# A hybrid decoder block: weight splits three tiles ahead for longer, nine attention units turned a slot later, sums of squares two slots behind the output

## The reference, cut to what matters

```python
u = rms_norm(h, norm1_w)                       # h: 16 meta tokens + 256 tokens, width 1024
proj = einsum('bld,dn->bln', u, w_in)          # a_q a_k a_v d_q d_k d_v d_gate d_beta d_a gate_a gate_d
y_a = differential_attention(a_q, a_k, a_v, lambdas, subln_w, lambda_init)
y_d = gated_deltanet(d_q, d_k, d_v, d_gate, d_beta, d_a, conv_w, A_log, dt_bias, norm_w)
mixed = sigmoid(gate_a) * (y_a @ w_branch_attn) + sigmoid(gate_d) * (y_d @ w_branch_dn)
h = h + mixed @ w_out
h = h + hierarchical_moe(rms_norm(h, norm2_w))  # 32 experts, the weights of all of them are read
out = rms_norm(h, final_norm_w)[:, 16:]

# differential attention, 8 heads, value width 128, blocks of 128 queries:
p = softmax(s + bias)                          # two maps per head
w = p[:, :, 0] - lam * p[:, :, 1]
o = einsum('bhqk,bkhe->bqhe', w, v)
o = rms_norm(o, subln_w) * (1 - lambda_init)   # needs the sum of squares of o per head and query
# DeltaNet inputs: d_q, d_k, d_v pass a causal convolution of 4 taps and SiLU
```

## Time and profile before

| | |
|---|---|
| median of 3 runs | 667.23 us (667.16 to 667.66) |
| the profiled execution | 665.98 us |
| its span in the profile | 664.2 us |
| TensorE busy | 601.6 us, 91% |
| VectorE busy | 327.4 us, 49% |
| ScalarE busy | 268.4 us, 40% |
| read from HBM | 154.12 MB |
| mean granted clock of TensorE | 0.972 |

### The profile page before, as it was taken

The page is one execution under the profiler, slowest core; times in us unless marked ns, Lnnn a source line. Parts: engine busy times, 40 slices in busy tenths (PEclk is TensorE's granted clock), DMA queues, the critical chain, the costliest instruction groups (busy, mean ns, idle before and its releaser), DMA issues.

```text
span 664.2 us, 14323 instructions
## 1 busy us (share of the span) xinstructions
PE 601.6 (91%) x5931; PEld 507.3 (76%) x5931; DVE 327.4 (49%) x693; ACT 268.4 (40%) x598; POOL 55.6 (8%) x102
## 2 busy tenths in 40 slices
PE   8999999899998799999999999999999677785874
PEld 8999989798988788899899999997554433444451
DVE  5344476878877568564765388624112110110112
ACT  6245567667776745333533575423110010100003
POOL 8300011101000002100220040000000000000000
PEclk9799999899999899999999999999999988997999
DMA  9744543233335331121312159999989999999994
GB/s 289 238 160 160 175 141 106 88 127 128 128 127 191 127 127 65 66 66 64 126 53 80 64 189 341 421 419 418 421 354 420 421 421 423 421 423 420 421 409 158
DMA packets 68560, 156.04 MB, mean 235 GB/s; under 512 B 4818, under 2 KB 54116, under 8 KB 56596
## 3 DMA queue, kind: packets, MB, share of 16 engines
q1 hardware_dynamic: 67136, 154.89, 61.4%
q0 software_dynamic: 176, 0.17, 0.2%
q10 hardware_dynamic: 1188, 0.12, 0.2%
HBM read 154.12 MB, written 1.05 MB: 234 GB/s over the span
## 4 chain that ended last, share of the span: by engine, by line
PE 45%; DMA 10%; SPq 9%; DVE 6%; ACT 5%; issue 3%; DVEq 0%; ACTq 0%
PE bank L850 19%; DMA arena<-in_expert_w_gate_dram 8%; SPq L521 6%; PE bank L1261 6%; PE bank L1037 5%; PE bank L835 3%; SPq L616 2%; DMA arena<-in_expert_w_down_dram 2%; PE bank L1015 2%; PE bank L1242 2%; PE bank L1286 1%; PE bank L1297 1%; DVE ring_lo L338 1%; ACT w_hi L333 1%; DVE arena L1909 1%
## 5 line engine op out<-in xcount | busy, mean ns | idle before, releaser
L850 PE MATMUL bank<-uT_hi,w_hi 128*128 128x272 f32 (+1 forms) x568 | 170.1, 299 | 4.6 <-ACT arena L1430 3.3
L850 PE MATMUL bank<-uT_lo,w_hi 128*128 128x272 f32 (+1 forms) x568 | 163.9, 289 | 0.0
L850 PE MATMUL bank<-uT_hi,ring_lo 128*128 128x272 f32 (+1 forms) x568 | 163.7, 288 | 0.0
L338 DVE TENSOR_TENSOR ring_lo<-arena,w_hi 128x1024 fp32r<-128x1024 f32 x88 | 107.6, 1226 | 48.0 <-ACT w_hi L333 47.4
L850 PEld LDWEIGHTS bank<-uT_hi,w_hi 128*128 128x128 f32 x568 | 109.1, 192 | 8.1 <-ACT w_hi L333 3.5
L850 PEld LDWEIGHTS bank<-uT_lo,w_hi 128*128 128x128 f32 x568 | 109.2, 192 | 0.2 <-issue 0.2
L850 PEld LDWEIGHTS bank<-uT_hi,ring_lo 128*128 128x128 f32 x568 | 109.2, 192 | 0.0
L333 ACT ACTIVATE w_hi<-arena 128x1024 fp32r<-128x1024 f32 x88 | 92.0, 1051 | 0.8 <-DMA arena<-in_w_in_dram 0.7
L1261 PE MATMUL bank<-arena 128*32 128x256 f32 x1024 | 63.7, 405 | 20.9 <-DMA arena<-in_expert_w_gate_dram 20.9
L1261 PEld LDWEIGHTS bank<-arena 128*32 128x32 f32 x1024 | 35.2, 116 | 44.4 <-issue 22.3
L1909 DVE SCALAR_TENSOR_TENSOR arena<-arena 128x272 f32<-128x272 f32 x72 | 36.0, 500 | 18.0 <-ACT arena L1423 17.4
(11 more groups left out here) (368 smaller groups left out, 1033.6 us busy)
## 6 DMA issues: line engine op xcount, KB each, us to landing
arena<-in_w_in_dram SPq DMA_DIRECT2D x36, 1024.0 KB, 5.0
arena<-in_expert_w_gate_dram SPq DMA_DIRECT2D x32, 1024.0 KB, 25.9
arena<-in_expert_w_up_dram SPq DMA_DIRECT2D x32, 1024.0 KB, 22.7
arena<-in_expert_w_down_dram SPq DMA_DIRECT2D x29, 1024.0 KB, 21.9
arena<-in_w_branch_attn_dram SPq DMA_DIRECT2D x4, 1024.0 KB, 5.1
arena<-in_w_branch_dn_dram SPq DMA_DIRECT2D x4, 1024.0 KB, 5.1
arena<-in_w_out_dram SPq DMA_DIRECT2D x4, 1024.0 KB, 8.4
arena<-in_expert_w_down_dram SPq DMA_DIRECT2D x6, 512.0 KB, 18.6
```

Of the source, the lines that this page charges most:

```text
L338: nc.vector.tensor_tensor(low_of(SPLIT[q]), src, w_hi[HI_OF[q]].bitcast(F32), ALU.subtract).then_inc(w_lo_ready, 1)
L850: last = pe.matmul(ps[:, 0:b.shape[2]], a[:, c, :], b[:, c, :], start=(c == 0 and i == 0), stop=(c == NC - 1 and i == 2))
```

## The change

Splits run three tiles ahead for n from 16 to 53 instead of 16 to 42. The fifth home serves until tile 55 instead of 44, and a tile takes the home whose last use is longest ago. The first expert load into slot 9 moves from behind unit 28 to behind unit 34. `out_high` waits for the last yd tile that used the homes in its area: tiles 80, 80, 88 and 87 done instead of 80, 80, 86 and 88.

Units 7 to 15 are turned three slots behind their own instead of two, and multiplied by the values four slots behind instead of three; units 0 to 6 stay. Keep and square of a head go with its output. The sums of squares come two slots behind the output instead of one.

```diff
-LONG_LEAD = range(FIRST["aq"], FIRST["dv"] + 3)
+LONG_LEAD = range(FIRST["aq"], FIRST["gate"] + 6)
...
-HI_OF = [q % (NSPLIT + 1) if q < FIVE_UNTIL else q % NSPLIT for q in range(len(SPLIT))]
+HI_OF = []
+for q in range(len(SPLIT)):
+    homes = range(NSPLIT + 1 if q < FIVE_UNTIL else NSPLIT)
+    HI_OF.append(min(homes, key=lambda i: max([p for p in range(q) if HI_OF[p] == i], default=i - NSPLIT - 1)))
...
+        TURN_SLOT = [m + (2 if i < 7 else 3) for i, m in enumerate(UNIT_SLOT)]
+        OUT_SLOT = [m + 1 for m in TURN_SLOT]
...
         def head_at(m):
-            i = unit_at(m)
+            i = unit_at(m, OUT_SLOT)
...
-                if u == FIRST["gate"] // 2 + 4:
+                if u == FIVE_UNTIL // 2 + 6:
...
-                if unit_at(m - 2) is not None:
-                    att_turn(unit_at(m - 2))
+                if m in TURN_SLOT:
+                    att_turn(unit_at(m, TURN_SLOT))
...
-                if unit_at(m - 3) is not None:
-                    att_out(unit_at(m - 3))
-                if head_at(m - 4) in (3, 7):
-                    att_ss(head_at(m - 4) // 4)
+                if m in OUT_SLOT:
+                    att_out(unit_at(m, OUT_SLOT))
+                if head_at(m - 2) in (3, 7):
+                    att_ss(head_at(m - 2) // 4)
...
-                if unit_at(m - 2) is not None:
-                    tr_out(("w", unit_at(m - 2)))
+                if m in TURN_SLOT:
+                    tr_out(("w", unit_at(m, TURN_SLOT)))
...
-                if head_at(m - 3) is not None:
-                    att_sq(head_at(m - 3))
+                if head_at(m) is not None:
+                    att_sq(head_at(m))
...
-                act.wait_ge(tile_ready, FIRST["yd"] + (0, 0, 6, 8)[i])
+                users = [n for n in SPLIT if HI_OF[n] < NSPLIT and HI_OF[n] // 2 == OUT_HI[i] - TSLOTS]
+                act.wait_ge(tile_ready, users[-1] + 1 if users else FIRST["yd"])
...
-                if head_at(m - 3) is not None:
-                    att_keep(head_at(m - 3))
+                if head_at(m) is not None:
+                    att_keep(head_at(m))
```

More of the change, by code:

```diff
@@ L381, in hybrid_block, with unit_at @@
         FIRST_SLOT = UNIT_SLOT[0]
-        def unit_at(m):
-            return UNIT_SLOT.index(m) if m in UNIT_SLOT else None
+        TURN_SLOT = [m + (2 if i < 7 else 3) for i, m in enumerate(UNIT_SLOT)]
+        OUT_SLOT = [m + 1 for m in TURN_SLOT]
+        def unit_at(m, slots=UNIT_SLOT):
+            return slots.index(m) if m in slots else None
         def head_at(m):
-            i = unit_at(m)
+            i = unit_at(m, OUT_SLOT)
             return i // TT if i is not None and i % TT == TT - 1 else None
@@ L403, in hybrid_block @@
         for m in range(FIRST_SLOT, SLOTS_A):
-            if unit_at(m - 2) is not None:
-                TR.append(("w", unit_at(m - 2)))
+            if m in TURN_SLOT:
+                TR.append(("w", unit_at(m, TURN_SLOT)))
             if m >= 16 + 2 and m - 2 < 24:
@@ L950, in key_sums @@
                 if 11 <= m <= 11 + H:
-                    turned = [key for key in TR if key[0] == "v" or key[0] == "w" and UNIT_SLOT[key[1]] + 2 < m or key[0] == "dv" and key[1] + 18 < m]
+                    turned = [key for key in TR if key[0] == "v" or key[0] == "w" and TURN_SLOT[key[1]] < m or key[0] == "dv" and key[1] + 18 < m]
                     pe.wait_ge(tr_copied, len(turned))
```

## The result

The changed kernel takes 658.73 us (median of four runs, 657.65 to 661.15), the kernel before 667.19 us beside it (four runs, 665.83 to 667.66): 8.5 us less by the medians. The ratio formed over all runs is 0.9883, interval [0.9856, 0.9910], which is 7.8 us less. The profiled execution took 661.15 us with a span of 659.4 us, so it is the slowest of the four.

A forecast was written before the change was run, and what follows sets the result against it. TensorE was taken to bound the kernel up to about 450 us, expert weight loads after. 5.2 + 1.24 - 1.0 - 0.4 = 5.0 us off the median 667.23 gave 662.2 us, range 659.8 to 664.6.

The forecast's parts named there:

- The ring does not get shorter: Rival, ScalarE and VectorE in the slots: ring stays at 4.21 us a slot; gain 3.3 us, 663.9 us; chance 0.18.
- The expert stage swallows it: Rival, expert stage: first loads bound by bandwidth, not finished tiles, so nothing comes through; 667.2 us; chance 0.05.
- Two short waits make one long one: Rival, dv turns: two waits of about a microsecond in one slot bring half clock; 1.5 us less gain, 663.7; chance 0.12.
- Parts 1 and 2: Slots with turns and sums of squares: waits of 1.73 and 1.97 us and 1.5 us of half clock go, 5.2 us.
- Part 2: Sums of squares two slots behind the output: the 1.97 us wait and 1.5 us of half clock behind it go.
- Part 3: dv turns, slots 18 and 19: dv 1 waits as before, dv 0 may wait too; 1.0 us lost.
- a ring that lags: At the dv turns: ScalarE and VectorE lag TensorE more than before, so the high end, 1.0 us lost, was taken.
- Part 4: Splits three tiles ahead until the sixth gate tile: two waits for low parts in slots 22 to 25 go, 1.24 us.
- Part 1: Units 7 to 15 turned a slot later: three waits before turns go, 1.73 us; ring needs about 4.0 us a slot.
- Part 5: Output tiles: third w_out copy waits for all eight yd tiles and delays the last mix copy; 0.4 us lost.
- its own low end: Whole kernel: nothing lost at the dv turns and the old 1.0 us there gone too; 7.4 us less, 659.8 us.

The follow-up runs named there:

- late_keep: Changed kernel with keep and square of a head a slot later, in slots without scores, and sums a slot later too; 664.42 us, ratio 0.9967.
- turn_only: Changed kernel with the short lead and early load again, keeping later turns, outputs and sums and the new choice of homes; 660.35 us, ratio 0.9920.
- late_square: Changed kernel with ScalarE's square of a head one slot later, behind the copy of turned weights, and the sums with it; 659.07 us, ratio 0.9901.
- roots_first: Changed kernel with the splits of tiles 53, 54 and 55 moved back on ScalarE and VectorE; 657.51 us, ratio 0.9870.
- again: The changed kernel, unaltered, run a second time beside the kernel before; 660.09 us, ratio 0.9902.
- sums_only: Kernel before with the sums of squares alone one slot later; 664.59 us, ratio 0.9977.

## Why the prediction was right and wrong

**The mechanisms held.** No wait before the sums of squares or before a turn, clock 1.00 from 110 to 190 us, no idle time at tiles 47 and 49, the 3.3 us wait unchanged, tile 88 longer by 0.45 us (forecast 0.4): each sign that the prediction named as right is in the profile. *The ring does not get shorter* is refuted: 4.01 us a slot, and late_keep, which undoes that, falls back to 110.55 us, 1.1 us less than before. *The expert stage swallows it* is refuted too: 447.4 us from tile 50 to the end in both. *Two short waits make one long one* did not come in the changed kernel, where dv 0 does not wait, but late_keep shows what it would have cost.

**The sizes, between tiles 24 and 50.** Parts 1 and 2 were put at 5.2 us. They can be checked by turn_only: 3.9 us, to which the new 0.8 at L948, the 0.3 more at the dv turns and the 0.3 more at tiles 47 and 49 are to be added, 5.3. They do not add up from single parts: the sums alone gave 2.0 where Part 2 had 3.5, because the turns stood right behind and came to wait in its place. The 1.5 us of half clock in Part 2 was not measured by itself, but its like was: with and without the fall behind tile 50's wait, tiles 50 to 60 take 58.72 and 57.37 us, 1.35 apart. The Trainium skill, TensorE: Matmul & The Clock Gate (Terms), would put it by an estimate at (1 - 0.61) x 4 + (1 - 0.97) x 4 = 1.7 us there, from granted clocks of 0.61 and 0.97 at 222 to 230 us; the measured length is again the smaller. Part 3 charged 1.0 us for a second wait at the dv turns; dv 0 does not wait at all, and dv 1 waits 1.3 where it was 1.0. Its reason, a ring that lags, was wrong for this kernel: the wait is the same with the ring relieved (late_square), and grows only where the ring is slower still (1.76 us in late_keep). Part 4 had 1.24 us and is worth 2.0 with the turns moved, 1.1 without. The 0.8 us at L948 was missed: Part 1 followed the keep on VectorE and counted the square in the ring, but did not ask what is queued behind the square on ScalarE. With these, 5.2 - 0.3 - 0.8 + 2.0 = 6.1 against 5.9 measured. Part 5 was right. All told the profiles gain 5.5 to 5.9 us where the sum said 5.0: the sum came close partly by luck, as Part 3 was put 0.7 too dear, Part 4 0.8 too cheap, and the 0.8 at L948 not at all.

**The step that failed** is the last of the sum: "The median of the runs, 667.23, lies 1.25 us above it; I subtract the same 5.0 us." The forecast missed 658.73 by 3.5 us, and most of this lies in the two medians and not in the change. The 78 executions of the kernel before, over all sets, have a median of 666.12 us (663.71 to 670.07), so the three runs from which I subtracted were 1.1 high. The ten executions of the changed kernel have 659.9 us (657.65 to 661.74), so the four that made the result were 1.2 low. Whether chance or the chip made these differences is not separated: the sets did not all run on the same chip, and their medians of the kernel before are 667.2, 666.6, 665.4, 666.3 and 665.3 us. Pooled, the change is worth 6.2 us by the medians and 6.6 by the means (666.18 against 659.61). Against 6.2 the sum of the parts was 1.2 short. Of this the profiles show 0.5 to 0.9. The rest stays open: the distance of two medians came out as 8.5, 6.6, 5.9 and 4.4 us in four pairs, two of them with the start edited, and that scatter is larger. No trace and no second set shows the 8.5 us: the largest of the others is 6.6. Beside the term, the range was too narrow below. It had room for unknown gains in the kernel (7.4 us at its own low end, 659.8), which pooled runs do not exceed, but none for a median of four that falls low beside a median of three that fell high.

## What to carry to other kernels

When two engines that serve TensorE go round in a ring (a tile's copy, taps, softmax, split, the next copy), look for the slot in which an extra step costs least. The same keep and square made the ring 0.2 us a slot longer when they stood in the slots without scores than in those with them, and that decided over 4.8 of 5.9 us in the profiles, 4.5 us by the medians. A wait that is removed was worth here only the distance to the next one: 3.5 us forecast, 2.0 had. The longer lead was worth 1.1 us alone, and with it two splits could be taken out of the way of a copy, 1.7 us, or 3.0 where the half clock goes too. That this needs the longer lead follows from the order of the splits; it was not run without it. Before a forecast is made to the microsecond, look at how far apart executions of one kernel lie: with a spread of 4 us, the median of three was 1.1 us high and that of four 1.2 us low, and both errors went the same way.

## What the runs showed of the hardware

Short waits close together were followed by half clock: 0.66 and 1.76 us of idle TensorE between 188.3 and 191.5 us in late_keep by a granted clock of 0.70 from 192 to 196 us (0.79 from 188), as 0.32 and 1.97 us had been by 0.61 in the earlier trace rows. The wait of 1.5 us in roots_first was not, nor were those of 1.3 us at the dv turn and 1.23 us at L963. The one of 3.3 us in front of tile 52 was, in ten profiles of 13. A block of 24 products with 16 columns, in which TensorE counts as busy, takes 4.13 us at full clock. In nine of the ten profiles with the block the granted clock falls, in seven before the block ends (it then takes up to 5.21 us) and in two behind it; 28 to 32 us has 0.54 in the changed kernel. Strewn among full products the same 24 were not followed by a fall in any of the seven profiles with that edit.

The granted clock does not tell all of the speed in the first microseconds. Ten filler products took 1.38 us in one profile (again) and 2.50 us in another (sums_only), behind the same idle time of 0.57 us, both with granted clock 1.00 from 4 to 12 us; the clock row of the profile's page would not have shown it. What made them slow stays open. In again:

```profile
6.64 0.66 PE L800 MATMUL bank<-arena 16*128 16x16 f32 x8 [0.57 <-DVE arena L1769]
7.23 1.38 PE L793 MATMUL bank<-arena 128*128 128x128 f32 x10
```

In sums_only:

```profile
6.63 1.03 PE L795 MATMUL bank<-arena 16*128 16x16 f32 x8 [0.57 <-DVE arena L1763]
7.59 2.50 PE L788 MATMUL bank<-arena 128*128 128x128 f32 x10
```
